# Pads of 96 to 480 bytes between a decoder kernel's activation buffers: what a buffer's place modulo 512 does to its matmuls

## The reference

```python
for i in range(2):
    h = rms_norm(x, attn_norm[i])
    proj = h @ w_in[i]                      # 1024 x 3072
    # stick-breaking attention (8 heads) and differential attention (4 heads)
    x = x + concat(sb, df) @ w_out[i]       # 1024 x 1024
    h2 = rms_norm(x, ffn_norm[i])
    if i == 0:
        x = x + (silu(h2 @ w_gate) * (h2 @ w_up)) @ w_down      # 1024 x 2816
    else:
        x = x + moe_swiglu(h2, ...)         # top 2 of 8 experts, 1024 x 3584 each
return rms_norm(x, final_norm)
```

## Time and profile before

| | |
|---|---|
| median of 3 runs | 1417.97 us (1417.54 to 1418.03) |
| profiled execution | 1417.77 us, of which the span from first to last instruction 1415.6 us |
| granted TensorE clock | 0.997 of 2.4 GHz |
| TensorE busy | 1400.8 us, 99% |
| VectorE busy | 1126.0 us, 80% |
| ScalarE busy | 935.7 us, 66% |
| moved from HBM | 429.74 MB |

### The profile page before, as it was taken

How to read it: one execution, slowest core, us unless ns; L and a number is a source line. 1 busy time by engine, 2 the same in 40 slices (tenths; PEclk the granted TensorE clock), 3 DMA queues, 4 the chain that set the end, 5 groups by cost and what they waited for, 6 DMA issues and landing times.

```text
span 1415.6 us, 18343 instructions
## 1 busy us (share of the span) xinstructions
PE 1400.8 (99%) x6929; PEld 1170.0 (83%) x6929; DVE 1126.0 (80%) x852; ACT 935.7 (66%) x758; POOL 37.1 (3%) x52
## 2 busy tenths in 40 slices
PE   8999999999999999999999999999999999999997
PEld 8888888889888888888888888888888888888885
DVE  6866445546856999888888888898888888889897
ACT  5555444335555877777777777777777777777775
POOL 0010000000010020000000000000000000001200
PEclk9999999999999999999999999999999999999999
DMA  9734985555434999999999999999999999999992
GB/s 334 260 115 148 396 305 183 185 181 179 149 93 161 352 392 394 396 393 386 364 395 382 360 384 385 373 365 391 389 346 397 382 360 385 390 378 355 396 395 109
DMA packets 190908, 448.81 MB, mean 317 GB/s; under 512 B 8515, under 2 KB 11402, under 8 KB 190858
## 3 DMA queue, kind: packets, MB, share of 16 engines
q1 hardware_dynamic: 188890, 441.74, 85.5%
q0 software_dynamic: 1648, 5.78, 1.1%
q10 hardware_dynamic: 320, 0.60, 0.1%
HBM read 429.74 MB, written 18.36 MB: 317 GB/s over the span
## 4 chain that ended last, share of the span: by engine, by line
PE 98%; DVE 1%; ACT 0%; DMA 0%; issue 0%; DVEq 0%; ACTq 0%
PE ps L515 90%; PE ps L971 2%; PE ps L642 1%; PE ps L600 1%; PE ps L673 0%; PE ps L520 0%; PE ps L930 0%; PE ps L696 0%; PE ps L631 0%; PE ps L806 0%; DMA cst<-in_consts 0%; PE ps L661 0%; PE ps L656 0%; PE ps L941 0%; PE ps L662 0%; PE ps L643 0%
## 5 line engine op out<-in xcount | busy, mean ns | idle before, releaser
L365 DVE TENSOR_TENSOR w_lo<-raw,w_hi 128x2048 fp32r<-128x2048 f32 x401 | 915.1, 2291 | 210.3 <-ACT w_hi L360 209.1
L360 ACT ACTIVATE w_hi<-raw 128x2048 fp32r<-128x2048 f32 (+1 forms) x401 | 766.9, 1914 | 304.4 <-PE ps L515 300.6
L515 PE MATMUL ps<-w_hi,xe_hi 128*128 128x512 f32 x896 | 247.1, 398 | 0.0
L515 PE MATMUL ps<-w_lo,xe_hi 128*128 128x512 f32 x896 | 241.8, 392 | 0.0
L515 PE MATMUL ps<-w_hi,xe_lo 128*128 128x512 f32 x896 | 240.9, 391 | 0.0
L515 PEld LDWEIGHTS ps<-w_lo,xe_hi 128*128 128x128 f32 x896 | 168.5, 188 | 37.2
L515 PEld LDWEIGHTS ps<-w_hi,xe_lo 128*128 128x128 f32 x896 | 168.4, 188 | 36.9
L515 PEld LDWEIGHTS ps<-w_hi,xe_hi 128*128 128x128 f32 x896 | 164.9, 188 | 32.7
L515 PE MATMUL ps<-w_hi,he_hi 128*128 128x512 f32 x448 | 122.2, 394 | 0.0
L515 PE MATMUL ps<-w_lo,he_hi 128*128 128x512 f32 x448 | 121.2, 392 | 0.0
L515 PE MATMUL ps<-w_hi,he_lo 128*128 128x512 f32 x448 | 120.8, 391 | 0.0
(11 more groups left out here) (244 smaller groups left out, 976.1 us busy)
## 6 DMA issues: line engine op xcount, KB each, us to landing
raw<-in_expert_w_gate SPq DMA_DIRECT2D x112, 1024.0 KB, 7.5
raw<-in_expert_w_up SPq DMA_DIRECT2D x112, 1024.0 KB, 7.8
raw<-in_expert_w_down SPq DMA_DIRECT2D x112, 1024.0 KB, 7.5
raw<-in_w_in SPq DMA_DIRECT2D x24, 1024.0 KB, 6.6
raw<-in_dense_w_gate SPq DMA_DIRECT2D x11, 1024.0 KB, 6.3
raw<-in_dense_w_up SPq DMA_DIRECT2D x11, 1024.0 KB, 8.1
raw<-in_dense_w_down SPq DMA_DIRECT2D x11, 1024.0 KB, 5.0
raw<-in_w_out SPq DMA_DIRECT2D x8, 1024.0 KB, 5.4
```

Source lines behind the costliest of these rows:

```text
L360: nc.scalar.activation(w_hi[:, n % SPL, first:PIECE], raw[:, n % RAW, first:PIECE], ACT.Copy).then_inc(hi_ready, 1)
L365: nc.vector.tensor_tensor(w_lo[:, n % SPL, :], raw[:, n % RAW, :], w_hi[:, n % SPL, :].bitcast(F32), ALU.subtract).then_inc(lo_ready, 1)
L515: return pe.matmul(o, stationary, moving, start=start, stop=stop, skip_group_check=True)
```

## The change

Eleven buffers `apart_0` to `apart_10`, which nothing reads or writes, are put between the others. No instruction is added or taken away. The diff's core:

```diff
         until_experts = ExitStack()
+        apart_0 = sb("apart_0", [P, 24], F32, until_experts)
         aT_hi = sb("aT_hi", [P, KT, S], F32R, until_experts)
+        apart_1 = sb("apart_1", [P, 112], F32, until_experts)
         aT_lo = sb("aT_lo", [P, KT, S], F32R, until_experts)
+        apart_2 = sb("apart_2", [P, 120], F32, until_experts)
...
+            apart_3 = sb("apart_3", [P, 96], F32, phase)
             hT_hi = sb("hT_hi", [P, FT, S], F32R, phase)
+            apart_4 = sb("apart_4", [P, 72], F32, phase)
             hT_lo = sb("hT_lo", [P, FT, S], F32R, phase)
...
+            apart_5 = se("apart_5", [P, 112])
             xe_hi = se("xe_hi", [P, KT, P], F32R)
+            apart_6 = se("apart_6", [P, 64])
             xe_lo = se("xe_lo", [P, KT, P], F32R)
+            apart_7 = se("apart_7", [P, 80])
...
+            apart_8 = se("apart_8", [P, 80])
             he_hi = se("he_hi", [P, 2, 4, P], F32R)
+            apart_9 = se("apart_9", [P, 112])
             he_lo = se("he_lo", [P, 2, 4, P], F32R)
+            apart_10 = se("apart_10", [P, 64])
```

## The result

| | before | after |
|---|---|---|
| median | 1417.76 us (4 runs) | 1432.88 us (1432.36 to 1433.33, 4 runs) |
| ratio | | 1.0104, 95% interval 1.0089 to 1.0119 |
| span of the profiled execution | 1415.6 us | 1429.9 us |

The pads make the kernel 15.1 us slower. The forecast was 1418 us, and the range ended at 1430.

What follows compares the result with a forecast made beforehand. TensorE, busy for 99% of the span, was taken as the bound, time being matmuls by pace. All terms were 0, so the span stayed 1415.6 us and the median was forecast at 1418 us, range 1402 to 1430.

Steps and rivals of the forecast that it cites:

- What bounds the kernel: Opening step: TensorE has 98% of the chain, so time is the number of matmuls by their pace.
- The terms of 0 for the writers and the transfers: Part-by-part terms: ScalarE's and VectorE's writes of moved halves are hidden, and transfers go into unmoved `raw`; each 0 us.
- the value of 0 ns for the 512-column matmuls: Main term: the new places leave all 5160 matmuls at their pace, chosen between 81.5 us less and 22.7 us more.
- the earlier trace shows two paces at one difference: First reason for 0: 117.5 and 113.1 ns at the same addresses modulo 512, so the difference does not choose.
- the other sign has 117.5 ns: Second reason for 0: with rows stationary, weights minus rows 64, 256 columns take exactly one of the two paces.
- steps of 512 bytes leave the pace alone: Third reason for 0: steps of 512 bytes and more between `aT`, `hT`, `xe` and `he` leave 229.1 ns.
- Loading beside streaming: Opening step: the next 128 x 128 block loads during streaming; if the reads collide, a pad alters the 15.8 ns excess.
- The slower one: Rival: some new differences are worse; half the matmuls at 4.4 ns more give 1429 us, all 1441; chance 0.20.
- The faster one: Rival: 448 is a bad difference; half the matmuls losing half the excess give 20 us, 1398; chance 0.22.
- Its far end: End of the faster rival: all the excess goes until the transfers stop it, 1344 us.
- The third: Rival that the change does nothing, 1418 us; 0.58 covers no dependence or one summing to less than 2.8 us.
- 256 columns: Term for the 864 short matmuls: some pieces change pace and others not, net 0, within 2 us.

Runs made afterwards that it cites:

- all_192: The kernel before with all eight halves at 192 in place of 448: 1418.23 us, ratio 1.0001.
- all_96: The kernel before with all eight halves at 96 behind the weights' halves in place of 448: 1447.32 us, ratio 1.0206.
- the scan: Computation left out, bare chains of matmuls differing only in where an operand lies: 226.67 ns for 512 columns at 0, 228.8 at 192.
- swapped: The changed kernel with xe given places 256 and 192 and he 384 and 128: 1429.77 us, ratio 1.0083.
- rows_0: The kernel before with xe, he and hT at 0 and aT left at 448: 1411.79 us, ratio 0.9953.
- rows_0_again: The same kernel with xe, he and hT at 0 and aT at 448, run in five more rounds: 1412.35 us, ratio 0.9955.

## Why the prediction was wrong, point by point

**What bounds the kernel: right.** TensorE has the chain before and after (98% and 99%), and time is count by pace. The clock's two levels are there in the trace of the kernel before as shares of 0.50 and 1.00. Two windows ahead of the expert stage (busy us by engine, granted clock, DMA share, GB/s):

```profile
441.00:442.00 1.00, 1.00 (x7) 1.00 (x6) 0.90 (x5) 1.00 (x1) 0.04 (x1) 0.50 0.24 45
445.00:446.00 1.00, 1.00 (x11) 1.00 (x10) 0.71 (x5) 0.83 (x2) 0.00 (x0) 1.00 0.00 0
```

By their start times in the trace the 128 x 128 float32 matmuls of line 520 follow each other after 213 to 215 ns at 0.50, and after 111 ns at 1.00. The terms of 0 for the writers and the transfers hold too: VectorE and ScalarE are busy for 1126.7 and 936.5 us beside 1126.0 and 935.7, and no wait for `raw` entered the chain. Pads by themselves cost nothing, as `all_192` shows (ratio 1.0001).

**The step that failed** is the value of 0 ns for the 512-column matmuls. The bounds given for it (15.8 ns less, 4.4 ns more) hold the measured +2.5 on average, and the choice between them was wrong. As bounds for any place they were off as well: with all halves at 96 it is +5.1 (`all_96`), and the best place gives back 2.4 of the 15.8. By kinds, from the traces before and after:

| matmuls | ns before | ns after | us |
|---|---|---|---|
| `xe`, 2688 | 229.1 | 232.5 | +9.1 |
| `he`, 1344 | 229.1 | 229.2 | +0.1 |
| `aT`, 864 of 512 columns | 229.1 | 232.7 | +3.1 |
| `hT`, 264 | 229.0 | 232.2 | +0.8 |
| 256 columns, 864 | 115.2 | 117.4 | +1.9 |
| sum | | | +15.0 |

The median moved by 15.1 us.

What the scan doesn't give is the pace where the two halves stand at different differences. With high rows in two of three matmuls its values would make 232.4 ns for `xe` (both halves at 128 modulo 256), 227.4 for `he` (0 and 192), 233.3 for `aT` (32 and 224) and 233.7 for `hT` (64 and 96). Measured are 232.5, 229.2, 232.7 and 232.2: right for `xe` alone, and off by 0.6 to 1.8 ns for the others. `swapped` has 229.6 for `xe` at 0 and 192 again. So a stream that goes from one difference to the other doesn't run at the mean of the two steady paces; why is not shown.

**Its reasons, one by one.** That the earlier trace rows shows two paces at one difference was read rightly, and the conclusion from it was not: that the start chooses a pace doesn't exclude that the difference chooses which paces there are. That the other sign has 117.5 ns, one of the same two paces, was taken for independence; it was a coincidence of the 256 columns: the scan has 117.8 at the difference of the earlier trace rows and 113.4 at that of the earlier trace rows, and its values run from 113.4 to 120.0. That steps of 512 bytes leave the pace alone was right, and says nothing about smaller ones. And a pad does alter what a matmul costs: with the same 128 x 128 block it is 226.7 or 234.2 ns by the block's start alone.

**Loading beside streaming.** The prediction has the next stationary block loaded while a matmul streams, and the trace of the kernel before has it so. The loads for the group that begins at 605.42:

```profile
605.19 0.87 PEld L515 LDWEIGHTS ps<-w_hi,xe_lo 128*128 128x128 f32 x4
```

The first of them begins 0.23 us before its own matmul, just as the one ahead starts, and a load takes 188 ns in the mean. What the place does beside this overlap depends on the type: nothing in bfloat16 (215.8 ns) and float32 (429.2), up to 7.5 ns on 226.7 in steps of 32 bytes in fp32r. That the two reads stand in each other's way is the author's conjecture; no run shows the reads themselves.

**The rivals.** The slower one named what came true: new places that are worse than 448, from 0.55 ns a matmul on. It was priced as half of the matmuls at +4.4 ns, 11.4 us; it is nearly three quarters of them (3816 of 5160) at +3.2 to +3.6, and the 256 columns besides, which the prediction took as net 0 within 2 us. The faster one, that 448 is a bad difference, is false: of the eight places in steps of 32 bytes only 0 is better. Its far end, an excess that goes altogether, doesn't occur at any place: at least 13.3 ns are left (226.6 in steps of 4 bytes). The third, by which nothing from 32 bytes upwards counts, is refuted by the same steps of 32 bytes, 226.7 to 234.2 ns.

**256 columns:** predicted net 0, measured +1.9 us, at the edge of the margin given.

## What to carry to other kernels

When fp32r operands of 512 columns stream back to back and TensorE is the bound, look at the distance of the starts, and place stationary and streamed operand at the same address modulo 256 (226.7 ns, beside 228.8 to 234.2 at the other steps of 32 bytes); if the stream has 256 columns, another difference is the best (the stationary operand 64 bytes behind the streamed one: 113.4 ns, beside 120.0 at 0). Here that was 6 us of 1418, and pads put in without a look at this cost 15 to 29. A parameter that the kernel never varies can't be judged from its trace: a scan of it as bare matmuls runs for 1.1 ms and would have given the sign.

## What the runs showed of the hardware that was not expected

- An fp32r matmul of 512 columns has 226.7 to 234.3 ns in steps of 32 bytes and up to 242.9 in steps of 4, with a period of 256 bytes. In float32 it is recorded as two of 429.2 ns and in bfloat16 as one of 215.8, at every place tried.
- At one difference there can be two paces: 228.7 to 229.1 and 233.3 to 233.4 ns at 192; at 64, with 256 columns, 113.1 and 117.5 in the kernel, 113.3 to 113.6 and 117.7 to 117.8 in bare chains.
- Narrowing the stationary block from 128 to 32 columns doesn't bring the distance of the starts under 226.7 ns; it changes which places are good (64 columns have 226.7 at 96, where 128 have 234.4).
- Runs of one kernel lie up to 3 us apart at the same work. In the stage with the router, TensorE's granted clock differs between profiled executions, as the windows from 400 to 460 us show for `rows_0`, then for the same kernel in `rows_0_again` (busy us by engine, granted clock, DMA share, GB/s):

```profile
400.00:460.00 60.00, 59.19 (x348) 50.94 (x349) 37.35 (x55) 32.02 (x36) 2.85 (x7) 1.00 0.36 119
```
```profile
400.00:460.00 60.00, 60.00 (x341) 52.55 (x341) 35.54 (x55) 30.71 (x34) 2.85 (x7) 0.94 0.33 107
```

  The spans were 1408.1 us and 1409.9; a difference of 2 us between two kernels has to be looked for in the chain's pieces, not in one span.
